# Who makes the low halves of V: every second group moved from GpSimd to VectorE, and sixteen casts moved from VectorE to ScalarE

## The chip, the cores and the metric

The kernel runs on one core of one Trainium2 chip. The time is that of the whole program on the device in microseconds (us), median over runs. One profiled execution stands beside the timed ones.

## What is computed

Two transformer blocks on 512 tokens of width 1024, all in float32. The first has recurrent and latent attention and a feed-forward layer of 4096. The second has retention, differential attention and, at its end, a retrieval over 16384 single-neuron experts (PEER). Only that last part is touched:

```
s = einsum('thpd,hpkd->thpk', q, subkeys)           # 8 heads, 2 halves, 128 keys each
s_top, i_top = top_k(s, 16)
c_top, c_idx = top_k(s_top[0] + s_top[1], 16)
e = take(i_top[0], c_idx // 16) * 128 + take(i_top[1], c_idx % 16)
g = softmax(c_top)
act = gelu(einsum('thkd,td->thk', u[e], x))
y = einsum('thk,thkd->td', g * act, v[e])
```

## The kernel before

TensorE multiplies in bf16: every float32 operand is split in a high half (a bf16 copy) and a low half (what the copy lost), and a product is three passes. So each weight tile that is streamed in has to be copied by ScalarE (high) and subtracted by another engine (low).

**Keys.** For each of 16 head halves n TensorE computes `half_query(n)` (24 matmuls, L1787) and, one behind, `scores_of(n-1)` (8 matmul passes, L2060). VectorE's `top16` (L2795 to L2805) finds the 16 best of 128 for the four token tiles, and signals `key_tops`. `scores_of(n)` waits for `key_tops` n-1, since two PSUM banks alternate. Behind each `top16` VectorE casts the 16 places to bf16 in pairs (`pair_up`, L2811). In this stage GpSimd makes the low halves of the last query weights (L821, 128x4096).

**Experts.** For tokens 128 to 511 all 16384 experts are computed densely, in 32 groups of 512 experts (a group is 4 tiles j). Tokens 0 to 127 instead gather their 128 rows of U and 128 rows of V each: GpSimd issues an indirect DMA for one row per token (`gather`, L937), VectorE takes it (`row_taken`, L2829 for U, L2833 for V). Four row buffers are in use, so gather n+4 waits until row n is taken. The activations of groups 0 to 13 (the *stored* ones) are computed early, without V. The loop looked at here then goes over i = 1 to 13, and each iteration computes the activations of the *live* group g = 14+i and applies V for two steps: the odd step 2i-1 and the even step 2i. Even steps below 28 belong to stored groups, odd ones to live groups. Four last groups g = 28 to 31 follow, one step each; I call them the tail. V's steps s are double-buffered by s % 2.

In an iteration each engine works through a fixed list:
- TensorE: 4 `live_tile` (24 matmuls, L2118), 8 `down` (18 matmuls, L2166), 8 `turn_fill` (4 transposes of U, L2108). A `turn_fill` waits until ScalarE has copied the previous one out (L1350, L1354).
- ScalarE: `v_high` (L1364) for both V steps, `live_gelu` (L1371), `live_high` (L1378) and `stored_high` (L1385), which wait for VectorE's products with the gates, and the two copies of each `turn_fill`. `v_high(s, j)` also waits until `down(s-2, j)` is done. One list, in order: a `live_high` that waits holds the copies behind it.
- VectorE: the products with the gates (`stored_times`, `live_times`, L2964), low halves of U (L2938) and of the activations (L2979, L2991), and 16 rows (i below 7) or 14.
- GpSimd: 8 `v_low` (L948, 128x1024) and 16 or 14 gathers, woven into each other in a fixed order.

`live_times(g, 0)` stands on VectorE behind the first three rows of the iteration; `live_high(g, 0)` on ScalarE waits for it, and the `turn_fill` after the third `live_tile` waits for ScalarE.

SyncE issues the loads. The next `load_v` into a buffer waits until all four `v_low` of the step are done.

Of the kernel before, what the change touches and what calls it, by code (L numbers as in the profile page):

```python
# [15 lines left out]
P = 128  # L16
T = 512
NT = T // P
D = 1024
# [93 lines left out]
def build(nc, ins, out):  # L113

    ctx = ExitStack()
    with ctx:
# [256 lines left out]
        late_in, keys_turned, keys_out = sem("late_in"), sem("keys_turned"), sem("keys_out")  # L373
# [10 lines left out]
        v_hi, v_lo, u_hi, u_lo = sem("v_hi"), sem("v_lo"), sem("u_hi"), sem("u_lo")  # L384
        index_ready, rows_taken = sem("index_ready"), sem("rows_taken")
# [133 lines left out]
        def _(sp):  # L519
# [210 lines left out]
            for i in range(EARLY):  # L730
# [5 lines left out]
                sp.wait_ge(v_lo, 4 * s + 4)  # L736
# [6 lines left out]
                sp.wait_ge(v_lo, 4 * (s + 1) + 4)  # L743
                load_v(s + 3)
            for s in range(2 * EARLY, EX_GROUPS - 2):
                sp.wait_ge(u_turned, 8 * (s - EARLY) + 8)
                load_u(s + 2)
                sp.wait_ge(v_lo, 4 * s + 4)
# [14 lines left out]
        def _(pool):  # L763
# [180 lines left out]
            def v_low(s, j):  # L944

                pool.wait_ge(v_hi, 4 * s + j + 1)
                at = slice(j * D, (j + 1) * D)
                pool.tensor_tensor(split[:, s % 2, 1, at], ring[:, s % 2, at], split[:, s % 2, 0, at], ALU.subtract).then_inc(v_lo, 1)  # L948

            pool.wait_ge(index_ready, 1)  # L950
# [6 lines left out]
            for i in range(EARLY):  # L957
                for m in range(8):
# [15 lines left out]
        def _(act):  # L974
# [301 lines left out]
            def keys_across(b):  # L1276

                act.wait_ge(keys_turned, b + 1)
                act.activation(keysT[:, 4 * b:4 * b + 4, :], bank(4 + b % 2).rearrange("p (g n) -> p g n", g=4), ACT.Copy).then_inc(keys_out, 1)
# [36 lines left out]

            for n in range(16):
# [5 lines left out]
                act.activation(half_q[:, n % 2, :], bank(2 + n % 2), ACT.Copy).then_inc(mm_out, 1)  # L1323
            def early_gelu(m):
# [63 lines left out]
            for m in range(SELECTED):  # L1388
                early_gelu(m)
                if m == 22:  # L1390
# [121 lines left out]
        def _(pe):  # L1512
# [492 lines left out]
            def turn_keys(b):  # L2005

                if b >= 2:
                    pe.wait_ge(keys_out, b - 1)
# [27 lines left out]
            pe.wait_ge(keys_out, 4)  # L2036
# [16 lines left out]
            def scores_of(n):  # L2053
                pe.wait_ge(mm_out, MM["wq"] + n + 1)
                if n == 0:
                    pe.wait_ge(keys_out, 4)
# [76 lines left out]
            for m in range(SELECTED):  # L2133
                if m in (2, 3):
                    pe.wait_ge(key_tops, 2 * P_HEADS - 3 + m)
                if m == SELECTED - 1:
                    for i, src in enumerate((pick_1, pick_2, pick_g)):
                        pe.wait_ge(picks_ready, i + 1)
# [30 lines left out]
            def hidden_here(s, j):  # L2169

                pe.wait_ge(v_lo, 4 * s + j + 1)
# [71 lines left out]
        def _(dve):  # L2243
# [565 lines left out]
            def pair_up(n):  # L2809

                own.did(dve.tensor_copy(top_pairs[:, :, n % 2, :, n // 2 * 2:n // 2 * 2 + 2],  # L2811
                                        top_i[:, :, n, :].unsqueeze(3).to_broadcast([P, NT, TOPK, 2])))

            for n in range(2 * P_HEADS):
                if n >= 1:
# [325 lines left out]
```

## Time and profile before

| | |
|---|---|
| median of 3 runs (2201.66, 2202.1, 2211.63) | 2202.1 us |
| profiled execution | 2197.33 us |
| its span, first to last instruction | 2195.5 us |
| busy: TensorE | 2077.8 us (95%) |
| VectorE | 1502.7 us (68%) |
| GpSimd | 1081.2 us (49%) |
| ScalarE | 827.5 us (38%) |

"Busy" of TensorE says that matmuls were in the array, not at which clock; a granted clock of 1.00 is 2.4 GHz, and 0.5 would be 1.2 GHz.

### The profile page before, as it was taken

The page shows a single profiled execution, that of the slowest core. Times are in us where ns is not written, and L with a number is a line of the kernel's source. Part 1 is how long each engine was busy: PE and PEld are TensorE (multiplying, and loading weights), DVE is VectorE, ACT ScalarE, POOL GpSimd, SP SyncE. Part 2 cuts the span into 40 slices and gives each one's busy share as a digit, 9 for nine tenths or more (in the row PEclk, how much of TensorE's full clock was granted, in tenths as well). Part 3 has the DMA queues.
Part 4 walks back from the last instruction along what each step waited for, and adds up shares of the span by engine and source line. Part 5 has one row for each costly group of instructions (what it writes and reads, how often), then busy time and mean ns, then how long its engine had stood idle before and what let it go on. Part 6 is the DMA issues. An engine that isn't in the chain of part 4 may idle for free.

```text
span 2195.5 us, 29225 instructions
## 1 busy us (share of the span) xinstructions
PE 2077.8 (95%) x11066; PEld 1147.8 (52%) x11218; DVE 1502.7 (68%) x2689; ACT 827.5 (38%) x1225; POOL 1081.2 (49%) x610
## 2 busy tenths in 40 slices
PE   8999899999989999889999988989999999999998
PEld 4446544444444456445666754545544555555554
DVE  2668555545541654695998968778887788888764
ACT  3232343323331444311137754333333434444442
POOL 1001346566545334861302227666666667677761
PEclk9999999999999999999999999999999999999999
DMA  7020438989974114996949999888887888888852
GB/s 236 0 105 12 154 117 242 258 245 248 254 224 150 66 53 137 252 295 170 329 155 390 379 339 344 307 309 309 311 306 286 306 304 302 307 308 285 317 185 83
DMA packets 277575, 514.90 MB, mean 235 GB/s; under 512 B 131122, under 2 KB 188726, under 8 KB 266436
## 3 DMA queue, kind: packets, MB, share of 16 engines
q1 hardware_dynamic: 232516, 367.90, 50.5%
q0 software_dynamic: 36864, 134.23, 17.8%
q10 hardware_dynamic: 8064, 11.01, 1.5%
q8 instruction: 83, 1.36, 0.2%
q14 instruction: 48, 0.39, 0.1%
HBM read 416.09 MB, written 67.65 MB: 220 GB/s over the span
## 4 chain that ended last, share of the span: by engine, by line
PE 25%; DVE 13%; DMA 11%; POOL 7%; issue 4%; ACT 1%; ACTq 0%; DVEq 0%; POOLq 0%; SPq 0%
PE ps L2166 8%; DMA arena<-in_peer_u,small 6%; PE ps L2091 6%; PE ps L2118 5%; DMA arena<-in_peer_v,small 4%; PE ps L2154 3%; POOL split L948 3%; POOL arena L937 3%; DVE arena L2829 2%; DVE x_sb L2833 2%; DVE arena L2938 2%; PE ps L2108 1%; DVE arena L2964 1%; DVE arena L2811 1%; PE ps L1787 1%
## 5 line engine op out<-in xcount | busy, mean ns | idle before, releaser
L2166 PE MATMUL ps<-split,arena 128*128 128x512 bf16 x1606 | 371.8, 384 | 4.8 <-DVE arena L2979 1.5
L948 POOL TENSOR_TENSOR split<-ring,split 128x1024 bf16<-128x1024 f32 x128 | 297.1, 2324 | 64.6 <-ACT split L1364 62.8
L2118 PE MATMUL ps<-arena 128*128 128x384 bf16 x1728 | 297.8, 330 | 10.6 <-ACT u_split L1371 9.9
L821 POOL TENSOR_TENSOR split<-ring,split 128x4096 bf16<-128x4096 f32 x26 | 207.2, 7969 | 193.3 <-ACT split L1146 191.0
L1787 PE MATMUL ps<-arena,split 128*128 128x512 bf16 x1316 | 296.5, 380 | 5.9 <-DVE arena L2610 2.0
L937 POOL DMA_INDIRECT arena<-in_peer_u,small x128 | 159.8, 1249 | 257.5 <-DVE arena L2829 240.2
L2166 PEld LDWEIGHTS ps<-split,arena 128*128 128x128 bf16 x1656 | 163.8, 99 | 186.4 <-issue 10.5
L2833 DVE SCALAR_TENSOR_TENSOR x_sb<-arena,small,x_sb 128x1024 f32<-128x1024 f32 x128 | 205.2, 1603 | 71.7 <-DMA arena<-in_peer_v,small 69.9
L2118 PEld LDWEIGHTS ps<-arena 128*128 128x128 bf16 x1728 | 170.4, 99 | 122.4 <-issue 17.5
L2829 DVE SCALAR_TENSOR_TENSOR arena<-arena,bcast 128x1024 f32<-128x1024 f32 x128 | 176.5, 1387 | 80.1 <-DMA arena<-in_peer_u,small 79.5
L1787 PE MATMUL ps<-split,arena 128*128 128x512 bf16 x1034 | 229.6, 381 | 1.2
L937 POOL DMA_INDIRECT arena<-in_peer_v,small x128 | 166.3, 1299 | 124.2 <-DVE x_sb L2833 103.2
L1787 PEld LDWEIGHTS ps<-arena,split 128*128 128x128 bf16 x1344 | 142.8, 107 | 151.5 <-DVE arena L2610 6.1
L1787 PEld LDWEIGHTS ps<-split,arena 128*128 128x128 bf16 x1056 | 103.6, 98 | 124.7 <-issue 1.9
L1146 ACT ACTIVATE split<-ring 128x4096 bf16<-128x4096 f32 x29 | 104.7, 3611 | 130.2 <-PE ps L1787 120.4
L2166 PE MATMUL ps<-split,u_split 128*128 128x512 bf16 x614 | 144.0, 384 | 2.1 <-issue 0.4
L1364 ACT ACTIVATE split<-ring 128x1024 bf16<-128x1024 f32 x128 | 134.4, 1055 | 30.4 <-PE ps L2166 19.8
L1350 ACT ACTIVATE arena<-ps 128x512 bf16<-128x512 f32 x144 | 86.0, 597 | 147.4 <-PE ps L2108 144.4
L826 POOL TENSOR_TENSOR u_split<-arena,u_split 128x1024 bf16<-128x1024 f32 x56 | 128.7, 2310 | 1.8
L2091 PE MATMUL ps<-arena,ring 128*128 128x384 bf16 x768 | 125.1, 326 | 0.0
L2108 PE MATMUL ps<-consts,ring 128*128 128x128 f32 x576 | 89.4, 279 | 35.7 <-ACT consts L1354 30.0
L2624 DVE TENSOR_TENSOR x_sb<-ps,x_sb 128x512 f32<-128x512 f32 x64 | 44.3, 692 | 108.9 <-PE ps L1787 108.9
(341 smaller groups left out, 3145.7 us busy)
## 6 DMA issues: line engine op xcount, KB each, us to landing
ring<-in_peer_v SPq DMA_DIRECT2D x32, 2048.0 KB, 12.8
ring<-in_peer_u SPq DMA_DIRECT2D x18, 2048.0 KB, 17.1
ring<-in_w_ff SPq DMA_DIRECT2D x16, 2048.0 KB, 8.6
arena<-in_peer_u SPq DMA_DIRECT2D x56, 512.0 KB, 4.8
turned_table<-u_split SPq DMA_DIRECT2D x56, 512.0 KB, 5.6
ring<-turned_table SPq DMA_DIRECT2D x14, 2048.0 KB, 10.4
gate_matrix<-split SPq DMA_DIRECT2D x12, 2048.0 KB
arena<-gate_matrix SPq DMA_DIRECT2D x32, 768.0 KB
```

Source lines behind the costliest of these rows:

```text
L821: pool.tensor_tensor(split[:, s4 % 2, 1, :], ring[:, (s4 + 5) % RING, :], split[:, s4 % 2, 0, :], ALU.subtract).then_inc(w_lo, 1)
L826: pool.tensor_tensor(pre_split[:, b, 1, :], pre_rows[:, b, :], pre_split[:, b, 0, :], ALU.subtract).then_inc(pre_lo, 1)
L937: pool.indirect_dma_start(row_buf[:, b, :], None, table[0], bass.IndirectOffsetOnAxis(row_index[:, k:k + 1], 0)).then_inc(row_in[b], 16)
L948: pool.tensor_tensor(split[:, s % 2, 1, at], ring[:, s % 2, at], split[:, s % 2, 0, at], ALU.subtract).then_inc(v_lo, 1)
L1364: act.activation(split[:, s % 2, 0, at], ring[:, s % 2, at], ACT.Copy).then_inc(v_hi, 1)
L1787: mm = pe.matmul(dst, a(k), b(k), start=n == 0, stop=n == len(terms) - 1)
L2091: mm = pe.matmul(early_bank(m), a, b, start=n == 0, stop=n == len(terms) - 1)
L2108: mm = pe.transpose(turn_to[:, k % 4, :], ring[:, u_place(g)[0], j * D + k * P:j * D + (k + 1) * P], ident)
L2118: mm = pe.matmul(up_bank, a, b, start=n == 0, stop=n == len(terms) - 1)
L2166: mm = pe.matmul(down_bank(t, c), a, w, start=s == 0 and j == 0 and n == 0, stop=s == EX_GROUPS - 1 and j == 3 and n == 2)
L2829: dve.scalar_tensor_tensor(row_buf[:, b, :], row_buf[:, b, :], 1.0, x_row, ALU.mult, ALU.mult, accum_out=dots[:, n:n + 1]).then_inc(rows_t ...
L2833: dve.scalar_tensor_tensor(x_sb[:, 0, :], row_buf[:, b, :], dots[:, n - PICKS:n - PICKS + 1], x_sb[:, 0, :], ALU.mult, ALU.add).then_inc(r ...
```

## The change

Three things. The low halves of V's odd steps are made by VectorE, those of the even steps stay with GpSimd; the counter `v_lo` becomes two, one for each. GpSimd keeps its gathers, now with half as many `v_low` between them. And the sixteen `pair_up` casts go from VectorE to ScalarE, three head halves later than before.

```
-            pool.wait_ge(index_ready, 1)
+            pool.wait_ge(picks_ready, 1)
...
                     gathers(n, n + more)
                     n += more
-                    v_low(2 * i + 1 + m // 4, m % 4)
-            for s in range(2 * EARLY + 1, EX_GROUPS):
+                    if m >= 4:
+                        v_low(2 * i + 2, m - 4)
+            for s in range(2 * EARLY + 2, EX_GROUPS, 2):
                 for j in range(4):
-                    gathers(n, n + 2)
-                    n += 2
+                    gathers(n, n + 4)
+                    n += 4
                     v_low(s, j)
...
+            def pair_up(n):
+
+                act.wait_ge(key_tops, n + 1)
+                act.activation(top_pairs[:, :, n % 2, :, n // 2 * 2:n // 2 * 2 + 2],
+                               top_i[:, :, n, :].unsqueeze(3).to_broadcast([P, NT, TOPK, 2]), ACT.Copy).then_inc(key_copies, 1)
...
                 act.activation(half_q[:, n % 2, :], bank(2 + n % 2), ACT.Copy).then_inc(mm_out, 1)
+                if n >= 3:
+                    pair_up(n - 3)
+            pair_up(13)
...
                 early_gelu(m)
+                if m < 2:
+                    pair_up(14 + m)
...
             for n in range(2 * P_HEADS):
-                if n >= 1:
-                    dve.wait_ge(key_tops, n)
-                    pair_up(n - 1)
...
+            def v_low(s, j):
+
+                if s >= EX_GROUPS or s % 2 == 0:
+                    return
+                dve.wait_ge(v_hi, 4 * s + j + 1)
+                at = slice(j * D, (j + 1) * D)
+                dve.tensor_tensor(split[:, s % 2, 1, at], ring[:, s % 2, at], split[:, s % 2, 0, at], ALU.subtract).then_inc(v_lo[1], 1)
...
                 stored_low(i, 0)
+                v_low(s + 1, 0)
...
                 stored_low(i, 2)
+                v_low(s + 1, 1)
...
                 rows_taken_to(n + 8, n + 10)
+                v_low(s + 1, 2)
                 live_times(g, 3)
...
                 u_low(f + 5)
+                v_low(s + 1, 3)
                 rows_taken_to(n + 12, n + 13)
```

The further `v_low` calls of the new code on VectorE with an even step return at once. SyncE, TensorE and the last wait of VectorE before `pair_keys(0)` read the new counters, with the same meaning.

How the lists change, at the places that the prediction speaks of. On ScalarE, in the stage of the keys, before (half queries, L1323, and high halves of the weights, L1146):

```order
L1323 ACTIVATE arena<-ps 128x512 [waits key_scores,mm_done] x2
L1146 ACTIVATE split<-ring 128x4096 [waits mm_done,ring_in2]
L1323 ACTIVATE arena<-ps 128x512 [waits key_scores,mm_done] x4
```

and with the change (L1330 is the half query, L1321 the cast):

```order
L1330 ACTIVATE arena<-ps 128x512 [waits key_scores,mm_done] x2
L1321 ACTIVATE arena<-arena 128x4x16x2 [waits key_tops]
L1147 ACTIVATE split<-ring 128x4096 [waits mm_done,ring_in2]
L1330 ACTIVATE arena<-ps 128x512 [waits key_scores,mm_done]
L1321 ACTIVATE arena<-arena 128x4x16x2 [waits key_tops]
```

The casts stand behind a copy of a half query, each with a wait for `key_tops`.

On VectorE in iteration 12, before: `live_times(g, 1)`, `live_low(g, 0)`, `stored_low(i, 1)`, a row of V, a low half of U, `stored_low(i, 2)`, a row.

```order
L2964 TENSOR_TENSOR u_split<-u_split,arena 128x384
L2991 TENSOR_TENSOR arena<-u_split,arena 128x384
L2979 TENSOR_TENSOR arena<-arena 128x384
L2833 SCALAR_TENSOR_TENSOR x_sb<-arena,small,x_sb 128x1024
L2938 TENSOR_TENSOR arena<-consts,arena 128x512
L2979 TENSOR_TENSOR arena<-arena 128x384
L2833 SCALAR_TENSOR_TENSOR x_sb<-arena,small,x_sb 128x1024
```

With the change (lines 4 further down, L3003 is the new `v_low`), from the same place:

```order
L2968 TENSOR_TENSOR u_split<-u_split,arena 128x384
L2995 TENSOR_TENSOR arena<-u_split,arena 128x384
L2983 TENSOR_TENSOR arena<-arena 128x384
L2836 SCALAR_TENSOR_TENSOR x_sb<-arena,small,x_sb 128x1024
L2942 TENSOR_TENSOR arena<-consts,arena 128x512
L2983 TENSOR_TENSOR arena<-arena 128x384
L3003 TENSOR_TENSOR split<-ring,split 128x1024
L2836 SCALAR_TENSOR_TENSOR x_sb<-arena,small,x_sb 128x1024
```

The second of the four new `v_low` stands behind the stored low half; all that follows on VectorE comes after it.

On GpSimd at the end of the loop and in the tail, before: the first row is `v_low(28, 2)` and `v_low(28, 3)`, the next four single ones are step 29, the last one is `v_low(30, 0)`.

```order
L948 TENSOR_TENSOR split<-ring,split 128x1024 x2
L937 DMA arena<-in_peer_v,small 128x1024 x2
L948 TENSOR_TENSOR split<-ring,split 128x1024
L937 DMA arena<-in_peer_v,small 128x1024 x2
L948 TENSOR_TENSOR split<-ring,split 128x1024
L937 DMA arena<-in_peer_v,small 128x1024 x2
L948 TENSOR_TENSOR split<-ring,split 128x1024
L937 DMA arena<-in_peer_v,small 128x1024 x2
L948 TENSOR_TENSOR split<-ring,split 128x1024
L937 DMA arena<-in_peer_v,small 128x1024 x2
L948 TENSOR_TENSOR split<-ring,split 128x1024
```

With the change, from the same place:

```order
L948 TENSOR_TENSOR split<-ring,split 128x1024 x2
L937 DMA arena<-in_peer_v,small 128x1024 x4
L948 TENSOR_TENSOR split<-ring,split 128x1024
L937 DMA arena<-in_peer_v,small 128x1024 x4
L948 TENSOR_TENSOR split<-ring,split 128x1024
```

Step 29 is gone from the list, and `v_low(30, 0)` is now the second row of this kind: ten gathers stood ahead of it, now four.

## Rows read from the trace of the kernel before

**Rows 1.** Windows, keys' stage: PE, PEld, DVE, ACT, POOL busy, PEclk, DMA share, GB/s

```profile
900.00:1000.00 100.00, 91.69 (x463) 49.51 (x472) 89.69 (x426) 21.02 (x21) 65.43 (x30) 0.97 1.02 287
```

**Rows 2.** Timeline of TensorE in the keys' stage (start, duration, line, idle before)

```profile
910.45 1.05 PE L2060 MATMUL ps<-arena 128*128 128x128 f32 x8
...
916.52 1.05 PE L2060 MATMUL ps<-arena 128*128 128x128 f32 x8
...
966.46 2.05 PE L2060 MATMUL ps<-arena 128*128 128x128 f32 x8 [6.37 <-DVE arena L2805]
...
1006.78 1.13 PE L2060 MATMUL ps<-arena 128*128 128x128 f32 x8 [1.09 <-DVE arena L2805]
```

**Rows 3.** Timeline of VectorE in the keys' stage

```profile
911.61 0.89 DVE L2795 MAX8 arena<-ps 128x8 f32<-128x128 f32 x4 [7.58 <-PE ps L2060]
...
916.87 0.33 DVE L2811 CAST arena<-arena 128x128 bf16<-128x128 uint32 x1
...
928.95 6.07 DVE L2811 CAST arena<-arena 128x128 bf16<-128x128 uint32 x1
...
953.67 7.50 DVE L2811 CAST arena<-arena 128x128 bf16<-128x128 uint32 x1
```

**Rows 4.** Timeline of GpSimd in the keys' stage

```profile
926.98 7.96 POOL L821 TENSOR_TENSOR split<-ring,split 128x4096 bf16<-128x4096 f32 x1 [6.68 <-ACT split L1146]
...
953.14 7.95 POOL L821 TENSOR_TENSOR split<-ring,split 128x4096 bf16<-128x4096 f32 x1
```

**Rows 5.** Windows of iterations 1 to 6, 7 to 9 and 10 to 13 of the experts' loop

```profile
1326.80:1669.20 342.40, 312.07 (x1604) 166.88 (x1633) 272.46 (x336) 132.02 (x220) 235.09 (x149) 0.96 0.86 311
1669.20:1833.10 163.90, 154.15 (x802) 82.92 (x816) 136.41 (x124) 66.00 (x110) 111.94 (x69) 0.97 0.83 294
1833.10:2037.60 204.50, 200.13 (x1070) 108.78 (x1089) 169.17 (x152) 86.37 (x144) 145.56 (x88) 1.00 0.86 305
```

**Rows 6.** Waits of TensorE from 1300 to 2180 us: total, times, longest

```profile
PE ps L2108 <- ACT consts L1354: 30.0, 10, 7.4
```

**Rows 7.** Timeline of TensorE at the start of iteration 7, around its stall

```profile
1669.23 4.06 PE L2118 MATMUL ps<-arena 128*128 128x384 bf16 x24
...
1682.13 1.12 PE L2108 MATMUL ps<-consts,ring 128*128 128x128 f32 x4 [4.51 <-ACT u_split L1354]
1683.04 5.87 PE L2118 MATMUL ps<-arena 128*128 128x384 bf16 x24
```

**Rows 8.** VectorE's rows of U (L2829), 1500 to 2100 us: ns min/median/max

```profile
L2829 DVE SCALAR_TENSOR_TENSOR arena<-arena,bcast x51: 1209/1215/3167, 1505.0 to 1678.2; 128x1024 f32<-128x1024 f32 x51
```

**Rows 9.** GpSimd's gathers (L937) in the same stretch

```profile
L937 POOL DMA_INDIRECT arena<-in_peer_v,small x116: 932/1206/1947, 1672.3 to 2096.0; - x116
```

**Rows 10.** The chain of waits from the end of iteration 6 into iteration 7

```profile
1655.13 2.38 POOL split L948
...
1661.68 2.14 POOL split L948
...
1665.24 12.93 DMA arena<-in_peer_u,small
```

**Rows 11.** Timeline of ScalarE in that stretch: `v_high` of the even step

```profile
1658.72 1.06 ACT L1364 ACTIVATE split<-ring 128x1024 bf16<-128x1024 f32 x1
```

**Rows 12.** Timeline of TensorE in the tail, group 29: first tile, fourth turn

```profile
2071.76 4.06 PE L2118 MATMUL ps<-arena 128*128 128x384 bf16 x24
...
2092.98 0.60 PE L2108 MATMUL ps<-consts,ring 128*128 128x128 f32 x4
```

**Rows 13.** Timeline of all engines in the tail, group 29

```profile
2078.12 1.95 POOL L937 DMA_INDIRECT arena<-in_peer_v,small  x1 [1.88 <-DVE x_sb L2833]
...
2079.16 0.55 DVE L2964 TENSOR_TENSOR u_split<-u_split,arena 128x384 f32<-128x384 f32 x1
...
2082.73 2.88 POOL L948 TENSOR_TENSOR split<-ring,split 128x1024 bf16<-128x1024 f32 x1 [0.41 <-ACT split L1364]
...
2090.70 1.28 DVE L2833 SCALAR_TENSOR_TENSOR x_sb<-arena,small,x_sb 128x1024 f32<-128x1024 f32 x1 [3.06 <-DMA arena<-in_peer_v,small]
```

More of the change, by code:

```diff
@@ L383, in build @@
         live_mul, live_hi, live_lo = sem("live_mul"), sem("live_hi"), sem("live_lo")
-        v_hi, v_lo, u_hi, u_lo = sem("v_hi"), sem("v_lo"), sem("u_hi"), sem("u_lo")
-        index_ready, rows_taken = sem("index_ready"), sem("rows_taken")
+        v_hi, v_lo, u_hi, u_lo = sem("v_hi"), [sem(f"v_lo{i}") for i in range(2)], sem("u_hi"), sem("u_lo")
+        rows_taken = sem("rows_taken")
         row_in = [sem(f"row_in{b}") for b in range(ROWS_AT_ONCE)]
@@ L947, in v_low @@
                 at = slice(j * D, (j + 1) * D)
-                pool.tensor_tensor(split[:, s % 2, 1, at], ring[:, s % 2, at], split[:, s % 2, 0, at], ALU.subtract).then_inc(v_lo, 1)
-            pool.wait_ge(index_ready, 1)
+                pool.tensor_tensor(split[:, s % 2, 1, at], ring[:, s % 2, at], split[:, s % 2, 0, at], ALU.subtract).then_inc(v_lo[0], 1)
+            pool.wait_ge(picks_ready, 1)
             pool.wait_ge(pre_lo, 4 * PRE)
@@ L2895, in _ @@
             pair_places(slice(0, 1))
+            dve.wait_ge(key_copies, 4 + 2 * P_HEADS)
             pair_keys(0)
-            dve.scalar_tensor_tensor(row_index, pick_1[:, 0, :], float(N_KEYS), pick_2[:, 0, :], ALU.mult, ALU.add).then_inc(index_ready, 1)
+            dve.scalar_tensor_tensor(row_index, pick_1[:, 0, :], float(N_KEYS), pick_2[:, 0, :], ALU.mult, ALU.add).then_inc(picks_ready, 1)
             for t in range(1, NT):
@@ L3003, in _ @@
             live_times(EARLY, 0)
+            v_low(0, 0)
             u_low(8)
+            v_low(0, 1)
             stored_low(0, 0)
             live_times(EARLY, 1)
+            v_low(0, 2)
             u_low(9)
+            v_low(0, 3)
             stored_low(0, 1)
@@ L3021, in _ @@
             u_low(12)
+            v_low(1, 0)
             live_low(EARLY, 2)
+            v_low(1, 1)
             rows_taken_to(27, 28)
@@ L3025, in _ @@
             live_low(EARLY, 3)
+            v_low(1, 2)
             rows_taken_to(28, 29)
             u_low(14)
-            rows_taken_to(29, 32)
+            v_low(1, 3)
+            rows_taken_to(29, 30)
+            v_low(2, 0)
+            rows_taken_to(30, 32)
+            v_low(2, 1)
             n = 32
@@ L3038, in _ @@
                 stored_times(i, 1)
+                v_low(s, 2)
                 rows_taken_to(n + 1, n + 2)
@@ L3042, in _ @@
                 u_low(f - 1)
+                v_low(s, 3)
                 rows_taken_to(n + 2, n + 3)
@@ L3070, in _ @@
                 u_low(f + 6)
+                v_low(s + 2, 0)
                 rows_taken_to(n + 13, n + 14)
@@ L3074, in _ @@
                     n += 2
+                v_low(s + 2, 1)
                 n += 14
@@ L3077, in _ @@
                 f = 8 * (g - EARLY) + 8
+                if g == 2 * EARLY:
+                    v_low(g, 2)
                 rows_taken_to(n, n + 2)
@@ L3080, in _ @@
                 u_low(f - 1)
+                if g == 2 * EARLY:
+                    v_low(g, 3)
                 rows_taken_to(n + 2, n + 3)
                 u_low(f)
+                v_low(g + 1, 0)
                 rows_taken_to(n + 3, n + 4)
@@ L3088, in _ @@
                 u_low(f + 2)
+                v_low(g + 1, 1)
                 rows_taken_to(n + 5, n + 6)
@@ L3094, in _ @@
                 u_low(f + 4)
+                v_low(g + 1, 2)
                 rows_taken_to(n + 7, n + 8)
@@ L3099, in _ @@
                 u_low(f + 6)
+                v_low(g + 1, 3)
                 live_low(g, 3)
```

27 lines of the change are left out of this document (12 added, 15 removed).

## The prediction, made before the change was run

> **What bounds the kernel now.** I read the page first: TensorE is busy for 95% of the span, so only its idle stretches, and stretches at a low clock, can be won. I then took windows stage by stage and the list of what TensorE waited for. Two places are touched by the change.
>
> *The keys.* TensorE is busy for 91.7 of 100 us there, while VectorE is at 89.7 [rows 1]. The eight-pass `scores_of` comes every 916.52 - 910.45 = 6.07 us, until it waits 6.37 us for VectorE's `top16`, and once more 1.09 us [rows 2]. The reason is on VectorE: one `top16` takes 916.87 - 911.61 = 5.26 us, which fits into 6.07, but the casts behind it, 0.33 us when all is quiet, took 6.07 and 7.50 us twice [rows 3]. Their ends, 935.02 and 961.17, are those of GpSimd's two long subtractions, 934.94 and 961.10 [rows 4]: the cast waits for GpSimd to let go of something both use.
>
> *The experts' loop.* In iterations 10 to 13, at granted clock 1.00, TensorE is busy for 200.13/4 = 50.0 us each [rows 5]; I take this as what an iteration needs at full rate. The windows show 342.4/6 = 57.1 us for iterations 1 to 6, 163.9/3 = 54.6 for 7 to 9 and 204.5/4 = 51.1 for 10 to 13 [rows 5]. What TensorE waits for is nearly always ScalarE's copy of a turned tile, 30.0 us in ten waits [rows 6]. Each idle stretch is paid for twice: behind the one of 4.51 us the turns took 1.12 us and the tile 5.87, against 4.06 for the same tile ahead of it [rows 7], about 2.3 us more; the granted clock of these windows is 0.96 and 0.97 of 2.4 GHz, that of iterations 10 to 13 is 1.00 [rows 5].
>
> ScalarE is late because its `live_high` waits for VectorE's `live_times`, and VectorE because of two things. It waits for rows: in the chain, GpSimd's `v_low` of an odd step (2.38 us), two gathers, a `v_low` of the even step, two more gathers, then 12.93 us of DMA [rows 10]. And some of its operations stretch: a row of U takes 1.215 us in the median, 3.167 at most [rows 8], and the long ones lie over a `v_low` of GpSimd.
>
> **The change part by part.**
>
> *Casts to ScalarE.* VectorE's need per head half falls to 5.26 us, below the 6.07 of TensorE, so both stalls go. Without them the fifteenth `scores_of` would start at 910.45 + 14 x 6.07 = 995.4 and the last some 1.1 us behind it, 996.5, against 1006.78 [rows 2]: 10.3 us. On ScalarE (21 of 100 us busy [rows 1]) sixteen casts of 128 elements cost 0.3 to 0.6 us each (an estimate; the nearest row is 1.06 us for 1024 elements, [rows 11]) and wait for a `key_tops` that is 5 us old by then; the next half query behind them is not held. What follows (early tiles, the last rows' splits, the picks) is released by TensorE's own progress, so the gain is kept. If the picks of the first tokens, which wait for GpSimd's sums, did not move with it, TensorE would wait at the gates instead, and 3 to 10 us would be left. I take 10.
>
> *V's odd low halves to VectorE.* The trace has no such operation on VectorE. The nearest is the row of U: two float32 inputs from SBUF, 1024 elements, 1.215 us unhindered and 3.167 at most [rows 8]. I take 1.2, since with half of the `v_low` gone from GpSimd little is left to hinder it; four per iteration are 4.8 us. Against that stand the stretches that odd `v_low` caused: at most 3.167 - 1.215 = 1.95 us each, 7.8 for four, at least nothing. VectorE's busy 272.5/6 = 45.4 us per iteration [rows 5] becomes 42.4 (between 42.4 and 50.2, and 7.8 more if every new one is stretched). GpSimd's 39.2 loses 4 x 2.14 to 2.38 [rows 10], to about 30.
>
> On the path: the odd `v_low` ahead of the gathers falls out. The even one cannot follow at once, it needs ScalarE's `v_high`, done at 1658.72 + 1.06 = 1659.8 [rows 11], against its start at 1661.68 [rows 10]. So the gathers behind it go out 1.9 us sooner, not 2.4 or more. At the start of the next iteration `live_times` loses one stretch of 1.95 us, as the `v_low` that lay over it was of an odd step. Together 3.8 us of a stall, and with the clock (4.51 us of idleness cost 2.3 more) about 5. The excess over 50.0 is 7.1 us in iterations 1 to 6, of which I take 4.6, as rows still take their 12.93 us of DMA: 28 us. In 7 to 9 it is 4.6, I take 2.7: 8 us. In 10 to 13 it is 1.1, I take 0.25 each: 1 us. Sum 37; the bounds are 9 x 1.3, about 12 (only a part of the path shortens and VectorE fills the rest with its new work), and all the excess, 61.
>
> Queued behind the new waits on VectorE are the rows and `live_times`. Each new `v_low` waits for a `v_high` that stands on ScalarE just ahead of what VectorE wants next anyway, so I cost these waits at nothing. If ScalarE's lead were gone, each would cost the 1.06 us of that copy. The load of the next odd V is released by VectorE's last `v_low`, behind `u_low(f + 5)`, perhaps 5 us later than now. It is hidden as long as the copy of that step isn't wanted for another 10 us.
>
> *GpSimd's order in the tail.* This part costs. Before, ten gathers stood between `v_low(28, 3)` and `v_low(30, 0)`, now four do (the order above). VectorE has taken row 225 when it enters group 28, so GpSimd stands at gather 230, and the four go up to 233: exactly those that group 28 uses. Group 29 needs 234 and 235 ahead of `live_times(29, 0)`. Before, these were on the way early, and `live_times` started at 2079.16 [rows 13]. Now they follow `v_low(30, 0)`, which waits for `v_high`, and that for `down(28, 0)` inside group 29. It ran from 2082.73; free of VectorE it takes 2.1, until 2084.9. The gathers go out at 2085 and 2086.3, and a gather took 2090.70 - 2078.12 = 12.6 us to its row [rows 13]: 2097.6 and 2098.9, the second row taken by 2100.1, `live_times` done by 2100.7. ScalarE's `live_high` and two copies make 1.6 more (an estimate from the same row: three short operations of half its length), so the turn that ran at 2092.98 [rows 12] can start at about 2102: a stall of 9 us, and 3 for the clock behind it. 12 us; the bounds are 4 (a gather in 6 us) and 15. Rows 238 and 239 come late too, but their `live_times` is then just in time.
>
> *Sum.* 10 + 37 - 12 = 35 us less. From the profiled 2197.3 us (2195.5 of span and 1.8 around it) that is 2162. The median of the timed runs lies 4.8 us above the profiled one, and I add it: **2167 us**.
>
> **A rule of the Trainium skill on the cast and on the gathers.** On the shared pair of ports, rows 3 and 4 show a cast that ends with GpSimd's operation. The Trainium skill, page "SBUF — State Buffer", section "SBUF: two separate sides", calls the pair "an **exclusive lock**, not a bandwidth split", held for a whole instruction; with the ends at 934.94 and 961.10 the trace agrees. The page adds that a VectorE operation with two SBUF inputs takes it only against a GpSimd operation that reads SBUF, by which the writing of gathers' descriptors would be free of the new `v_low`: the sum would stay as it is. The trace bears it out only in part: a gather's issue takes 932 ns at least, 1206 in the median and 1947 at most [rows 9]. If issues do wait for two-input operations, that is a rival, below.
>
> **Rivals.**
> 1. *Full recovery.* The tail's gathers land sooner than 12.6 us and the chain gives back most of the excess of 61: 10 + 50 - 6 gives 2148. For it: iterations 10 to 13 already run at 51.1 with the same eight `v_low`. Chance 0.17.
> 2. *Only the first link shortens.* The even `v_low` and the DMA stay where they are, VectorE fills what it wins: 12 us in the loop, 10 in the keys, 12 lost in the tail, 2192. For it: half the gathers are still behind `v_high`. Chance 0.16.
> 3. *Gather issues wait for the new operations.* 1.0 us each (1947 - 932) on one or two gathers of the path in nine iterations, 14 us: 2181. Chance 0.1.
> 4. *Slower: VectorE becomes the bound.* If each new `v_low` is itself stretched to 3.2 us and the old stretches stay with the remaining ones, an iteration holds 45.4 + 12.7 = 58.1 us of VectorE and some row waiting. It decides as soon as VectorE needs more than the 57.1 us of iterations 1 to 6. At 60 us for each of 13 iterations the loop takes 780 us instead of 711: 69 - 10 + 12 = 71 slower, 2273; at 57, 30 slower, 2232. Against it: stretches need a GpSimd operation in progress, and there are half as many. Chance 0.08.
> 5. *Nothing in sum.* Gains and the tail's loss cancel, 2202, if the tail costs 15 twice (rows 238 too) and the loop gives 12. Chance 0.07.
>
> The case of the sum has the rest, 0.42.
>
> **How the numbers follow.** A difference under 0.5%, 11 us, can't be told from none. Below 2191 lie the sum, rivals 1 and 3 and half of rival 2: 0.77 to 0.8. Within 11 us: the other half of 2 and rival 5, 0.13. Slower: 0.08. The range 2143 to 2196 leaves out rival 4, most of 5 and the far end of 1.
>
> **What would show it.** The casts on ScalarE under 0.6 us, TensorE's `scores_of` every 6.07 us up to the last one, and the first early tile 10 us sooner. In the windows, iterations 1 to 6 near 52.5 us and clocks of 0.98 or more; new `v_low` on VectorE near 1.2 us. In group 29 one TensorE wait of some 9 us for ScalarE's copy, with `v_low(30, 0)` ahead of the gathers of rows 234 and 235. I am wrong if VectorE's busy time per iteration rises above 48 us, if the iterations don't get shorter, or if group 29 has no stall.

## The result, and the profile after

| | before | changed |
|---|---|---|
| median, same chip | 2208.05 us (6 runs) | 2156.57 us (6 runs, 2151.36 to 2159.07) |
| ratio, 95% interval | | 0.977 (0.9744 to 0.9796) |
| profiled execution | 2197.33 us | 2156.65 us |

The changed kernel is faster by 51 us in the medians and by 40.7 us between the two profiled executions: that of before was a short one. One of the six runs of before took 3642.46 us and the ratio leaves it out; without it the median of before is 2204.46 and the difference 48 us. In a later comparison (the last run below) it was 2155.99 against 2199.86, ratio 0.9796 (0.9776 to 0.9815). Places in the program are compared between the profiled executions.

The page of the changed kernel, busy time of the engines:

```profile
PE 2072.5 (96%) x11066; PEld 1147.4 (53%) x11218; DVE 1415.4 (66%) x2737; ACT 831.2 (39%) x1241; POOL 961.0 (45%) x546
```

VectorE got 64 operations of 1.22 us more and was 1502.7 us busy before. Now it is 1415.4. That is the line to stop at: it was handed work and became less busy. The sixteen casts that left it made up 22.1 us, so that by its own work it should be at 1558.7.

Windows of the changed kernel (PE, PEld, DVE, ACT, POOL busy, PEclk, DMA share, GB/s): keys, iterations 1 to 6, 7 to 9, 10 to 13.

```profile
900.00:1000.00 100.00, 99.02 (x509) 54.89 (x520) 80.23 (x461) 26.56 (x40) 63.33 (x28) 0.98 1.03 282
1319.00:1631.60 312.60, 303.02 (x1604) 163.21 (x1632) 241.26 (x363) 132.40 (x220) 173.75 (x122) 0.99 0.92 334
1631.60:1791.00 159.40, 152.85 (x802) 82.86 (x816) 124.07 (x135) 66.11 (x110) 98.20 (x58) 0.98 0.89 321
1791.00:1991.70 200.70, 199.65 (x1069) 108.96 (x1088) 149.66 (x168) 86.51 (x144) 125.02 (x72) 1.00 0.87 314
```

Against [rows 1, 5]: 52.1 us per iteration in place of 57.1, 53.1 in place of 54.6, 50.2 in place of 51.1, together 38 us; TensorE's granted clock in the first two stretches is 0.99 and 0.98 of 2.4 GHz where it was 0.96 and 0.97. VectorE's busy time per iteration fell from 45.4 to 241.26/6 = 40.2 us, although 4.9 us are new. GpSimd's fell from 39.2 to 29.0.

TensorE's timeline in the keys' stage, the first and the last rows of `scores_of` (the last row holds two of them):

```profile
913.17 1.05 PE L2072 MATMUL ps<-arena 128*128 128x128 f32 x8
919.24 1.05 PE L2072 MATMUL ps<-arena 128*128 128x128 f32 x8
...
992.09 1.05 PE L2072 MATMUL ps<-arena 128*128 128x128 f32 x8
998.16 2.01 PE L2072 MATMUL ps<-arena 128*128 128x128 f32 x16
```

They come every 6.07 us without a wait. The last starts about 86.0 us behind the first; before it was 96.33 [rows 2]: 10.3 us. The first one is 2.7 us later than before, with no edit ahead of it that adds work; over all kernels of this study it started between 907.3 and 914.6, so I take this for scatter and leave it out of every comparison below. With it the places add up: 2.7 later, 10.3 less in the keys, 38 less in the loop and 5.1 more in the tail (below) make 40.5 of the 40.7 us.

ScalarE's casts in all, from the line's own view (ns min/median/max):

```profile
L1321 ACT ACTIVATE arena<-arena x16: 308/311/319, 926.0 to 1009.6; 128x128 bf16<-128x128 uint32 x16
```

Not one is stretched, while GpSimd's long subtractions run beside them.

What TensorE waited for from 1300 to 2180 us (total, times, longest), the stretch of [rows 6]:

```profile
PE ps L2130 <- ACT u_split L1381: 6.7, 4, 4.1
PE ps L2120 <- ACT u_split L1364: 5.8, 1, 5.8
PE ps L2120 <- ACT consts L1364: 4.4, 6, 3.2
PE ps L2178 <- DVE arena L2983: 1.4, 1, 1.4
```

The first of these rows is TensorE waiting at a `live_tile`, the next two at a `turn_fill`. The 30.0 us at `turn_fill` under "consts" are 4.4; under "u_split" there were 5.7 us before and are 5.8. All rows together were 43.0 us and are 18.3. Two of the waits that are left are singled out. The 5.8 us is the start of iteration 7, here on ScalarE, GpSimd and VectorE:

```profile
1643.09 0.31 ACT L1457 ACTIVATE small<-small 128x128 f32<-128x128 f32 x1 [16.98 <-DVE arena L2832]
```
```profile
1624.28 2.13 POOL L948 TENSOR_TENSOR split<-ring,split 128x1024 bf16<-128x1024 f32 x1 [0.83 <-ACT split L1374]
...
1628.62 1.43 POOL L937 DMA_INDIRECT arena<-in_peer_u,small  x1 [0.30 <-issue]
```
```profile
1641.83 1.23 DVE L2832 SCALAR_TENSOR_TENSOR arena<-arena,bcast 128x1024 f32<-128x1024 f32 x1 [6.16 <-DMA arena<-in_peer_u,small]
```

ScalarE stands for 17 us at the one operation that needs all 128 rows of U, and holds its copies back. The last two gathers of U go out at 1626.56 and 1628.62, behind the `v_low` of an even step, and the last row is taken 13.2 us after the second of them.

The other is the tail, group 29, on TensorE, GpSimd and VectorE:

```profile
2043.25 4.06 PE L2130 MATMUL ps<-arena 128*128 128x384 bf16 x24
2050.47 0.66 PE L2120 MATMUL ps<-consts,ring 128*128 128x128 f32 x4 [3.16 <-ACT consts L1364]
2051.23 5.47 PE L2178 MATMUL ps<-split,arena 128*128 128x512 bf16 x17
2056.54 0.60 PE L2120 MATMUL ps<-consts,ring 128*128 128x128 f32 x4
2056.98 4.06 PE L2130 MATMUL ps<-arena 128*128 128x384 bf16 x24
```
```profile
2036.90 2.13 POOL L948 TENSOR_TENSOR split<-ring,split 128x1024 bf16<-128x1024 f32 x1 [27.41 <-ACT split L1374]
2039.18 0.97 POOL L937 DMA_INDIRECT arena<-in_peer_v,small  x1
2040.45 0.94 POOL L937 DMA_INDIRECT arena<-in_peer_v,small  x1 [0.30 <-issue]
```
```profile
2045.65 2.71 DVE L2836 SCALAR_TENSOR_TENSOR x_sb<-arena,small,x_sb 128x1024 f32<-128x1024 f32 x2 [15.77 <-DMA arena<-in_peer_v,small]
```

`v_low(30, 0)` stands 27.4 us waiting, with the two gathers that group 29 needs behind it. VectorE waits 15.8 us for the rows, and TensorE 3.16. Its tiles then stand 13.73 us apart where 8.66 is the rule: 5.07 us lost. 3.16 of them are the wait; most of the rest is the `down` behind it, 5.47 us in place of 3.83, in a stretch (2051.2 to 2056.7) with a granted clock of 0.70.

### The profile page after: what moved, and what is told of

It reads as the page before. It is cut to its first block, busy times and chain, and to the rows that moved or that the text cites. A ratio compares the mean times of both kernels' runs of the same rounds, so it can differ in the third digit from the quotient of the medians.

```text
span 2154.8 us, 29226 instructions
## 1 busy us (share of the span) xinstructions
PE 2072.5 (96%) x11066; PEld 1147.4 (53%) x11218; DVE 1415.4 (66%) x2737; ACT 831.2 (39%) x1241; POOL 961.0 (45%) x546
## 3 DMA queue, kind: packets, MB, share of 16 engines
q1 hardware_dynamic: 232516, 367.90, 51.7%
## 4 chain that ended last, share of the span: by engine, by line
PE 38%; DMA 10%; DVE 5%; POOL 3%; issue 3%; ACT 1%; POOLq 0%; ACTq 0%; DVEq 0%; SPq 0%
PE ps L2178 13%; DMA arena<-in_peer_u,small 9%; PE ps L2130 8%; PE ps L2103 6%; PE ps L1799 4%; PE ps L2166 3%; DVE arena L2832 2%; PE ps L2120 2%; POOL split L948 1%; POOL arena L937 1%; PE ps L2141 1%; PE ps L2142 1%; PE ps L2072 1%; DVE arena L2968 1%; DVE arena L2942 1%
## 5 line engine op out<-in xcount | busy, mean ns | idle before, releaser
L937 POOL DMA_INDIRECT arena<-in_peer_u,small x128 | 160.7, 1255 | 301.2 <-DVE arena L2832 288.3
L2836 DVE SCALAR_TENSOR_TENSOR x_sb<-arena,small,x_sb 128x1024 f32<-128x1024 f32 x128 | 184.4, 1441 | 110.3 <-DMA arena<-in_peer_v,small 108.7
L937 POOL DMA_INDIRECT arena<-in_peer_v,small x128 | 196.4, 1535 | 116.3 <-DVE x_sb L2836 101.2
L2832 DVE SCALAR_TENSOR_TENSOR arena<-arena,bcast 128x1024 f32<-128x1024 f32 x128 | 165.5, 1302 | 83.7 <-DMA arena<-in_peer_u,small 83.5
L948 POOL TENSOR_TENSOR split<-ring,split 128x1024 bf16<-128x1024 f32 x64 | 146.6, 2292 | 114.3 <-ACT split L1374 113.5
L1349 ACT ACTIVATE split<-ps 128x1024 f32<-128x1024 f32 x48 | 94.9, 1980 | 38.9 <-PE ps L2142 37.0
## 6 DMA issues: line engine op xcount, KB each, us to landing
ring<-turned_table SPq DMA_DIRECT2D x14, 2048.0 KB, 10.3
```

The source lines that it names most:

```text
L937: pool.indirect_dma_start(row_buf[:, b, :], None, table[0], bass.IndirectOffsetOnAxis(row_index[:, k:k + 1], 0)).then_inc(row_in[b], 16)
L2832: dve.scalar_tensor_tensor(row_buf[:, b, :], row_buf[:, b, :], 1.0, x_row, ALU.mult, ALU.mult, accum_out=dots[:, n:n + 1]).then_inc(rows_t ...
L2836: dve.scalar_tensor_tensor(x_sb[:, 0, :], row_buf[:, b, :], dots[:, n - PICKS:n - PICKS + 1], x_sb[:, 0, :], ALU.mult, ALU.add).then_inc(r ...
```

## The experiments

All ratios are against the kernel before on the same chip, with the 95% interval. Experiments 1 to 3 and the first run of 7 were made on one chip, the others on a second one. For each kernel I give the length of iterations 1 to 6 (from the starts of their first live tiles) and of the tail, which I measure from the first tile of group 28 to the last tile of all (127.26 us before).

**1. The casts alone.** The kernel before, with this part of the change only:

```diff
-            pair_up(n - 1)                   # VectorE, behind top16(n - 1)
+                if n >= 3:                   # ScalarE, behind the copy of half query n
+                    pair_up(n - 3)
```

> The kernel before with only the sixteen casts moved to ScalarE; all low halves of V stay on GpSimd. My theory: the two waits of TensorE for the top-16 (6.4 and 1.1 us) vanish, scores_of comes every 6.07 us to the end, and the whole program gains 10 us (0.3 to 0.6%); the experts' loop stays at about 57 us per iteration in iterations 1 to 6. Rival: the time won at the keys is lost again at the gates or in the first iterations of the loop, so that the program gains under 3 us.

Measured: 2194.64 us, ratio 0.995 (0.9934 to 0.9966), 12.5 us less in the medians. The last `scores_of` starts 86.0 us behind the first, as in the changed kernel. Iterations 1 to 6 take 57.4 us. The keys are worth what was forecast. What follows loses nothing that the medians show; the loop's 57.4 us beside 57.1 before come from single executions.

**2. V's low halves alone.** The changed kernel with the casts put back on VectorE:

```diff
-                if n >= 3:
-                    pair_up(n - 3)           # ScalarE
+                if n >= 1:
+                    dve.wait_ge(key_tops, n)
+                    pair_up(n - 1)           # VectorE
```

> The changed kernel with the casts put back on VectorE; only the low halves of V's odd steps moved. My theory: 38 us less in the loop, 5 us more in the tail, 33 us less in all against the kernel before (ratio about 0.985); one or two casts of 6 to 7 us at the keys are back. Rival (the two parts work on each other, or the casts give more than the keys' 10 us): the gain is under 25 us.

Measured: 2162.62 us, ratio 0.9823 (0.9798 to 0.9849); iterations 1 to 6 take 52.1 us. 0.995 x 0.9823 = 0.9774 is the whole change's 0.977: the parts add up. The ratio is a little below the 0.985 forecast; the tail is 133.53 us long, 6.3 more than before. The casts are held again, VectorE's timeline, and GpSimd's beside it:

```profile
922.67 0.23 DVE L2812 CAST arena<-arena 128x128 bf16<-128x128 uint32 x1
928.75 6.05 DVE L2812 CAST arena<-arena 128x128 bf16<-128x128 uint32 x1
...
957.18 4.95 DVE L2812 CAST arena<-arena 128x128 bf16<-128x128 uint32 x1
```
```profile
926.76 7.95 POOL L821 TENSOR_TENSOR split<-ring,split 128x4096 bf16<-128x4096 f32 x1 [6.25 <-ACT split L1147]
954.09 7.96 POOL L821 TENSOR_TENSOR split<-ring,split 128x4096 bf16<-128x4096 f32 x1
```

GpSimd's operations end at 934.71 and 962.05, the casts at 934.80 and 962.13.

**3. The tail in its old order.** The changed kernel with

```diff
-            for s in range(2 * EARLY + 2, EX_GROUPS, 2):
-                for j in range(4):
-                    gathers(n, n + 4)
-                    n += 4
-                    v_low(s, j)
+            gathers(n, n + 8)
+            n += 8
+            for j in range(4):
+                gathers(n, n + 2)
+                n += 2
+                v_low(2 * EARLY + 2, j)
```

> The changed kernel with GpSimd's old order in the tail: ten gathers ahead of v_low(30, 0), and two ahead of each further one. My theory: the stall of 3.2 us at the turn of group 29 and the slow matmuls behind it vanish, the tail gets 5 us shorter, the rest is unchanged: 5 us below the changed kernel. Rival (the stall comes from the latency of the DMA or from VectorE's new work and not from the order): no difference.

Measured: 2153.07 us, ratio 0.9756 (0.9729 to 0.9782). The tail is 127.26 us long, as before, against 132.33 in the changed kernel: 5.07 us. The medians differ by 3.5 us, which the intervals don't separate; the tail's length and the missing stall do. The place in the list is what counts here, and neither VectorE's new work nor the length of `v_low`: with the first cut (experiment 5) the tail still takes 131.96 us, with the second (experiment 6) 131.75.

**4. GpSimd's old list with stand-ins.** Does the loop's gain come from GpSimd's relief, and from what of it? In these three kernels GpSimd gets its old order back (in the tail too), with something in each place of an odd step's `v_low`; VectorE keeps its new operations.

```diff
-                    if m >= 4:
-                        v_low(2 * i + 2, m - 4)
+                    (v_low if m >= 4 else stand_in)(2 * i + 1 + m // 4, m % 4)
...
+            def stand_in(s, j):
+                pool.wait_ge(v_hi, 4 * s + j + 1)
+                own.wait()
+                own.did(pool.tensor_tensor(scratch, bcast[:, 0:D], bcast[:, 0:D], ALU.subtract))
```

4a, the subtraction above, 128x1024:

> The changed kernel, but GpSimd has its old list back, with a stand-in at each place of an odd step's v_low: the same wait for v_high and a subtraction of 128x1024 from a constant tile into a free one. VectorE keeps its new operations. My theory (the loop's gain is GpSimd's relief): iterations 1 to 6 are back at 57 us or more, since VectorE's operations are stretched as before and it has 4.9 us more to do; the program at 2195 to 2240 us. Rival (the gain comes from the place of the new operations on VectorE, not from GpSimd): it stays within 10 us of the changed kernel.

4b, the same of 8 columns:

> The same with stand-ins of only 8 columns: the old waits for v_high in GpSimd's list stay, its time and its hold on the memory ports go. If the time and the port matter, as I think: iterations 1 to 6 at 52 to 54 us, the program within 12 us of the changed kernel. Rival (the waits for ScalarE's v_high in front of the gathers were the cost): 56 us or more, the program at 2190 us or above.

4c, in its place

```diff
-                own.did(pool.tensor_tensor(scratch, bcast[:, 0:D], bcast[:, 0:D], ALU.subtract))
+                for _ in range(4):
+                    own.wait()
+                    own.did(pool.memset(scratch, 0.0))      # 128x512
```

> Stand-ins that fill 128x512 four times (some 2.1 to 2.8 us in all) in place of the subtraction: the old waits and the old time of GpSimd stay, but it reads nothing from SBUF. Theory A (what costs is mostly that VectorE's two-input operations are held while GpSimd reads): no VectorE operation is stretched by a stand-in, and iterations 1 to 6 take 52 to 55 us. Theory B (what costs is that the gathers are issued later): as the run with full stand-ins, 57 us or more. I give A 0.5.

Measured:

| | median us | ratio | iterations 1 to 6 |
|---|---|---|---|
| 4a, subtraction | 2188.25 | 0.9937 (0.9919 to 0.9956) | 57.7 us |
| 4b, 8 columns | 2151.85 | 0.9766 (0.9733 to 0.9800) | 52.7 us |
| 4c, fills | 2157.63 | 0.9800 (0.9769 to 0.9832) | 52.6 us |

The windows of iterations 1 to 6, of 4a, then 4b, then 4c:

```profile
1316.94:1663.31 346.37, 313.39 (x1605) 166.85 (x1632) 300.86 (x366) 130.67 (x220) 230.56 (x148) 0.95 0.83 299
```
```profile
1317.27:1633.34 316.07, 303.26 (x1604) 163.21 (x1632) 239.79 (x363) 132.62 (x220) 191.74 (x147) 0.99 0.91 332
```
```profile
1320.33:1635.87 315.54, 303.84 (x1604) 163.68 (x1632) 244.79 (x363) 132.12 (x220) 244.99 (x225) 0.99 0.91 331
```

The fifth and the seventh figure decide (VectorE, GpSimd). In 4c GpSimd is busier than in 4a, 40.8 us per iteration against 38.4, waits for the same signals in the same order and issues its gathers behind them, and the loop is as fast as with 8 columns. What differs is that a fill reads nothing, and that VectorE is busy for 40.8 us per iteration instead of 50.1. So neither the waits nor GpSimd's time ahead of the gathers cost anything to speak of; what costs is that VectorE stands still while GpSimd reads. 4a was forecast at 57 us or more per iteration, which it took, and at 2195 us or more in all, which it stayed below; 4b and 4c are within their forecasts. The stand-ins themselves, 4a and 4c (ns min/median/max):

```profile
L955 POOL TENSOR_TENSOR arena<-bcast x64: 1899/1905/3549, 1309.3 to 2134.0; 128x1024 bf16<-128x1024 f32 x64
```
```profile
L956 POOL MEMSET arena<- x256: 524/524/550, 1312.7 to 2103.9; 128x512 f32 x128
```

A fill is never longer than 550 ns, the subtraction up to 3549: it is held by VectorE too. A fill lasts only a quarter of a `v_low`, so one might think that it holds VectorE too, only more briefly. VectorE's timeline in 4c rules this out. From 1300 to 2130 us, 204 of its two-input operations that are listed singly lie over a fill and over no subtraction, and all of them have their undisturbed times (128x384 at most 0.55 us, 128x512 at most 0.69, 128x1024 at most 1.28). Those over a subtraction reach 3.02, 3.14 and 5.0 us. By the same count 143 operations lay over a subtraction in the kernel before, and 55 do in the changed one. 4b and 4c have a tail of 127.3 us, a second sign that the tail's loss was the order's.

**5. VectorE's new work cut.** In the changed kernel the new `v_low` on VectorE is `j * D : j * D + 8` from step 3 on.

> The changed kernel with VectorE's new v_low cut to 8 columns from step 3 on (the low halves of V's odd steps are left out, so its output is not the reference's; waits and signals stay). My theory (VectorE's 4.9 us per iteration are hidden under TensorE): within 4 us of the changed kernel. Rival (VectorE is late by them): iterations 1 to 6 near 50.5 us and the program 6 us or more below the changed kernel.

Measured: 2154.20 us, ratio 0.9786 (0.9756 to 0.9815), iterations 1 to 6 at 51.8 us against 52.1. The new work is hidden, as forecast. VectorE's busy time fell by only 2.1 us per iteration (228.38/6 = 38.1), not by the 4.9 that were cut: the `v_low` left on GpSimd now met other operations, `u_low` of the one half with 1270 ns in the mean in place of 889 and the row of U with 1401 in place of 1327 (iterations 1 to 6).

**6. GpSimd's remaining low halves cut.** The same on GpSimd, from step 2 on.

> The changed kernel with the v_low that GpSimd keeps (even steps) cut to 8 columns from step 2 on, waits and signals kept (the low halves of V's even steps are left out, so its output is not the reference's). If what is left over the full rate in iterations 1 to 6 (52.1 against 50.2 us) comes from these operations: 50.2 to 51.5 us, and the program 5 to 15 us below the changed kernel. Rival (it comes from the rows' DMA alone): no change above 3 us. VectorE's operations should all be at their undisturbed times.

Measured: 2146.37 us, ratio 0.976 (0.9735 to 0.9785); iterations 1 to 6 at 309.51/6 = 51.6 us, of which iteration 1 alone has 58.3 and the other five 50.3; iteration 7 has 52.7 in place of 59.1. The median is 9.6 us below the changed kernel's on this chip, as forecast. The forecast range for 1 to 6 was missed by a little, and for a reason that it didn't name: iteration 1 is another case, while 2 to 6 are at full rate. The row of U is at 1220 ns in the mean and `u_low` at 683, their undisturbed times. VectorE is busy for 218.35/6 = 36.4 us per iteration: the four `v_low` that GpSimd keeps cost it 40.2 - 36.4 = 3.8 us, 0.95 each.

**7. All low halves on VectorE.** The calls for the even steps are in the changed kernel already; this takes the early return away and the `v_low` out of GpSimd's list.

```diff
-                if s >= EX_GROUPS or s % 2 == 0:
+                if s >= EX_GROUPS:
...
-                    if m >= 4:
-                        v_low(2 * i + 2, m - 4)
```

> All low halves of V on VectorE; GpSimd does only the gathers from the loop on. My theory (what still stalls TensorE is gathers behind v_low on GpSimd): VectorE's busy time rises from 40.2 us per iteration (1 to 6) to 44 or 45, still below 50.2, iterations 1 to 6 take 50.5 to 51.5 us in place of 52.1, the 59 us of iteration 7 become 51 to 56, the tail's stall goes; 10 to 20 us below the changed kernel. Rival (VectorE is what is late, and its further work delays the products with the gates): iterations above 52.5 us and the program 5 to 40 us slower than the changed kernel.

> All low halves of V on VectorE, a second time, for comparison on the same chip: ratio 0.970 to 0.974.

Measured: 2143.58 us, ratio 0.9716 (0.9691 to 0.9740), and on the other chip 2140.57 us, 0.9729 (0.9710 to 0.9749), where the changed kernel had 0.9796 (0.9776 to 0.9815). It is the version that beats both, by some 15 us beside the changed kernel on one chip. From its view of groups by line and from its windows (iterations 1 to 6):

```profile
L2995 DVE TENSOR_TENSOR split<-ring,split 128x1024 bf16<-128x1024 f32 x122 | 148.9, 1221 | 35.5 <-ACT split L1366 35.5
```
```profile
1321.17:1633.79 312.62, 303.55 (x1634) 163.52 (x1632) 249.56 (x398) 131.16 (x219) 120.73 (x100) 0.99 0.93 340
```

All eight `v_low` of an iteration are on VectorE, 9.8 us, and it is busy for 41.6 us, less than in the kernel before without any, and less than the forecast 44 or 45. Iterations 1 to 6 take 52.1 us, not the forecast 50.5 to 51.5: iteration 1 has 59.1, the other five 50.7. Iteration 7 is at 50.2, the tail at 127.26. On the other chip it was 51.7, 51.3 and 127.25.

Against the changed kernel VectorE is busier by 1.4 us per iteration, so that this second step is not won by VectorE's time. Most of the 15 us lie where gathers had stood behind a `v_low`: the tail is 5 us shorter and iteration 7 by 6 (second chip) or 9 us.

**8. Rows taken earlier.** On top of 7, to see whether iteration 1 can be had too:

```diff
-            rows_taken_to(20, 23)
+            rows_taken_to(20, 27)
             for j in range(4):
                 stored_times(0, j)
```

and each later `rows_taken_to` of the first iteration four rows ahead.

> All low halves of V on VectorE, and in the first iteration VectorE takes four rows more ahead of its wait for the gates (rows 20 to 26 in place of 20 to 22), so that the gathers behind them go out during the 17 us of that wait and each later row of the iteration is taken one or two places earlier. My theory (iteration 1 is late because its first rows are): the 59.0 us of iteration 1 become 50 to 54, the program 5 to 9 us below the kernel with all low halves on VectorE. Rival (the products of the gates in the first iteration come later by it, or the lead is lost again): no gain, or up to 5 us slower.

Measured: 2137.79 us, ratio 0.9724 (0.9705 to 0.9744), not to be told from 7 on the same chip (0.9729). Iteration 1 is at 50.2 us, 8.8 less. But the loop starts later, by a wait of TensorE for VectorE's low half just ahead of it:

```profile
1303.86 6.48 PE L2170 MATMUL ps<-split,arena 128*128 128x512 bf16 x17 [7.68 <-DVE arena L2975]
```

From the fifteenth `scores_of` to iteration 1 it is 331.3 us against 320.7 in 7: 10.6 lost for 8.8 won in iteration 1 and 0.6 behind it. The forecast gain of 5 to 9 us did not come. The rival's first half was right. Counted from the first `scores_of`, VectorE's first `live_times` comes 392.2 us behind it against 384.3 in 7, and with it that low half. But the rows are not what makes it late: VectorE is through with them at 1289.2 and then waits for the transfer of the gates, here for `stored_times` and for `live_times`:

```profile
1292.98 1.96 DVE L2960 TENSOR_TENSOR arena<-arena 128x384 f32<-128x384 f32 x4 [3.80 <-DMA arena<-gate_matrix]
1299.44 0.56 DVE L2960 TENSOR_TENSOR u_split<-u_split,arena 128x384 f32<-128x384 f32 x1 [4.49 <-DMA arena<-gate_matrix]
```

Why these gates land later than in 7 stays open.

**9. The changed kernel again**, for comparison on the chip of 6 to 8:

> The changed kernel again, on the same chip: ratio 0.975 to 0.980; iterations 1 to 6 at 51.5 to 52.7 us.

Measured: 2155.99 us, iterations 1 to 6 at (1634.30 - 1319.80)/6 = 52.4 us, the tail at 132.19.

## Why the prediction was right, and where its reasons were not

| term | forecast | measured |
|---|---|---|
| keys | -10 | -10.3 |
| iterations 1 to 6 | -28 | -29.8 |
| 7 to 9 | -8 | -4.5 |
| 10 to 13 | -1 | -3.8 |
| tail | +12 | +5.1 |
| profiled execution | 2162 | 2156.65 |
| median | 2167 | 2156.57 |

*Keys.* Right in place, mechanism and size, shown by experiments 1 and 2: the cast on VectorE ends with GpSimd's subtraction, the cast on ScalarE never waits. The gain stays to the end.

*Loop.* The size was right and its reason half wrong. The forecast put together 1.9 us of earlier gathers, 1.95 us for one stretched operation and the clock's share. The first of these is worth nothing measurable: 4c keeps the waits and the busy time ahead of the gathers and is as fast. The waits of the new operations for `v_high`, which I had put at nothing, came to 1.3 us in all from 1300 us on. The step that failed is the one that priced the stretches, "at most 3.167 - 1.215 = 1.95 us each, 7.8 for four", read from the row of U alone. It led to VectorE's 42.4 to 50.2 us per iteration; measured are 40.2. The same stretches lay on other operations, where I had not looked. Groups by line, 1320 to 2130 us (busy, mean ns), before and then of the changed kernel:

```profile
L2938 DVE TENSOR_TENSOR arena<-consts,arena 128x512 bf16<-128x512 f32 x63 | 93.4, 1483 | 4.3 <-ACT consts L1354 4.3
L2964 DVE TENSOR_TENSOR u_split<-u_split,arena 128x384 f32<-128x384 f32 x63 | 66.8, 1060 | 5.9 <-ACT u_split L1371 5.9
```
```profile
L2942 DVE TENSOR_TENSOR arena<-consts,arena 128x512 bf16<-128x512 f32 x66 | 50.0, 758 | 5.6 <-ACT consts L1364 5.5
L2968 DVE TENSOR_TENSOR u_split<-u_split,arena 128x384 f32<-128x384 f32 x68 | 37.6, 553 | 13.7 <-ACT u_split L1381 13.6
```

The `u_low` of the one half of a tile (shown) took more than twice its 0.68 us in the mean, that of the other half 1.03 us, and `live_times` almost twice its 0.55. In the kernel before the groups' means would have shown this: their medians are 0.682 and 0.548 us, and here a mean far above the median was held time. The four odd `v_low` of GpSimd cost VectorE 45.4 + 4.9 - 40.2 = 10.1 us per iteration, 2.5 each, where doing them itself costs 1.22 each. Experiment 4 gives the same sum a second time (50.1 against 40.0 in 4b). The four even ones, which are left, cost it 0.95 each (experiment 6): a `v_low` has no fixed price as interference, it depends on which operations it meets.

The Trainium skill, page "SBUF — State Buffer", section "SBUF: two separate sides", has the rule by which VectorE's two-input operations block against "a GpSimd op that reads SBUF". The fills of 4c, which read nothing, bear out that condition: VectorE's busy time there is within 1 us per iteration of that with 8 columns, and no two-input operation that met only fills is longer than its undisturbed time. I had cited the rule for the cast and for the gathers, and had not priced by it the other operations on VectorE's list.

*7 to 9 and 10 to 13.* Iteration 7 stayed at 59.1 us (57.1 before), since the last gathers of U stand there behind an even `v_low`, and ScalarE waits for them. Experiment 6 cuts the length of those and keeps their waits, and iteration 7 falls to 52.7; 7 takes them off GpSimd's list, and it falls to 50.2 (51.3 on the second chip). Both changes also free VectorE, and no run separates that from the gathers. The iterations after it are all at 50.17 or 50.18.

*Tail.* The mechanism was right, shown by 3: four gathers in place of ten ahead of `v_low(30, 0)`, one stall in group 29. Only its size was off. I took 12.6 us from gather to row, from a busy stretch; here no gather had been issued for 30 us, and the row came 2045.65 - 2039.18 = 6.5 us after its issue. I had put that case at the lower bound, 4 us; it was 5.07.

*Median.* I added 4.8 us for the distance of the median from the profiled execution of before. The changed kernel has none (2156.57 and 2156.65), and that is half of the 10 us by which I forecast too high.

*Rivals.* VectorE never became the bound: it got freer. Gather issues did get longer in the V half, 1383 ns in the median against 1206 [rows 9], and it is the new operations that do it: with them cut (experiment 5) the median is 1218. So the second half of the rule, as the prediction read it, doesn't hold here: an issue is not free of VectorE's two-input operations. But the price is 0.2 us, and the loop shows no loss by it; 1 us on the path is excluded by the length of the iterations, 50.17 us in 10 to 13.

*Sums.* Two of the prediction's numbers are off without bearing on the forecast: rival 4 at 57 us per iteration gives 30 - 10 + 12 = 32 us slower, not 30, and half of rival 2 with rival 5 is 0.15, not 0.13.

What stays open is iteration 1, 56 to 63 us in every kernel but that of experiment 8, where the time is lost one place ahead, to the gates' transfer.

## What to carry to other kernels

When two engines hold each other off, count an operation's cost on both. Here 2.1 us on the free engine cost 2.5 us on the busier one for the operations that were moved, and the busier one could do it in 1.2; for those that stayed it cost 0.95, so count again after each step. Before moving work off a loaded engine, compare the mean of every group on it with its median: where the operations of a group have one shape, a mean far above the median points at held time, and the timeline tells what held them. And an operation that waits, in the list of an engine that also issues transfers, must stand behind those that the next stage needs: when a list gets thinner, its old spacing has to be counted again.

## What the runs showed of the hardware

- VectorE with two inputs in SBUF and GpSimd's subtraction hold each other for whole operations, whichever started first: in the tail of the changed kernel GpSimd's own `v_low` took 4.50 us (2.13 alone) at 2051.45, over a row of VectorE's operations.
- GpSimd's fill of 128x512 did not hold VectorE's two-input operations and was not held by them: 524 to 550 ns in 256 fills, and 204 operations of VectorE over fills at their undisturbed times (4c).
- GpSimd's issue of a gather is lengthened by such operations and doesn't lengthen them. In the changed kernel, behind 1500 us, 24 issues with VectorE idle took 0.93 to 0.97 us, those over its operations up to 2.76 us, while VectorE's operations over issues alone kept their times (155 of 128x384 at most 0.56 us).
- ScalarE's cast of 128x128 from uint32 to bf16 took 308 to 319 ns beside GpSimd's 7.96 us subtraction; the same cast on VectorE took 228 to 277 ns in its faster half and up to 7.50 us beside it (kernel before).
- A gather's row was taken 6.5 us after its issue when no other gather had been issued for 30 us, and 13.2 us after it at the end of iteration 6, behind five others within 14 us; from issue to landing it was 4.2 us at least, 7.7 in the median and 14.9 at most (changed kernel, 1500 to 2100 us).
